# Fixing expert 0 as the first item of a mixture-of-experts stage, with its weights loaded ahead of the routing

## The reference, cut to what matters

```python
mod = jax.nn.silu(c) @ w_mod[l] + b_mod[l]          # six vectors of 1024: shift, scale, gate, twice
x = x + gate1 * rms_norm(hybrid_mixer(h, ...), g_post_mix[l])
h = rms_norm(x, g_pre_ffn[l]) * (1.0 + scale2) + shift2
logits = (xt @ router_w + router_b)                  # 256 x 32
top_v, top_i = lax.top_k(logits, 4)
gates = jax.nn.softmax(top_v, axis=-1)
# for each expert e, over the rows idx that picked it:
gu = xb @ w_gate_up[e] + b_gate_up[e]
act = x_glu * jax.nn.sigmoid(1.702 * x_glu) * (x_lin + 1.0)
out += gate * (act @ w_down[e] + b_down[e])
x = x + gate2 * rms_norm(y, g_post_ffn[l])
```

## Time and profile before

| | |
|---|---|
| median of 3 runs | 2647.13 us (2645.96 to 2648.38) |
| the profiled execution | 2651.04 us, its span 2648.6 us |
| mean granted TensorE clock | 0.98 of full speed |
| PE, DVE, ACT busy | 2439.9, 1115.0, 825.8 us |
| MoE weights moved | 384 loads of 1 MB |
| first MoE load issued | at 259.5 us of the span |
| last item's result read | at 1280.0 us |

### The profile page before, as it was taken

The page is one execution under the profiler, slowest core; times in us unless marked ns, Lnnn a source line. Parts: engine busy times, 40 slices in busy tenths (PEclk is TensorE's granted clock), DMA queues, the critical chain, the costliest instruction groups (busy, mean ns, idle before and its releaser), DMA issues.

```text
span 2648.6 us, 31931 instructions
## 1 busy us (share of the span) xinstructions
PE 2439.9 (92%) x10826; PEld 1504.6 (57%) x10826; DVE 1115.0 (42%) x1597; ACT 825.8 (31%) x1227; POOL 147.2 (6%) x212
## 2 busy tenths in 40 slices
PE   8997899999988888888899999899999999999999
PEld 4755333323222222222488777677887887777787
DVE  4556011110111111111455676856556556887554
ACT  2321111111111111111344345434443444345443
POOL 0000010110100010010000000000000000100000
PEclk9998899999999999999999999999999999999999
DMA  8754999999999999999565562453655655534554
GB/s 308 265 183 131 349 411 421 418 421 402 420 421 421 420 411 408 407 413 410 181 202 185 181 194 80 152 198 109 197 186 167 197 185 190 156 119 164 162 188 145
DMA packets 263485, 700.39 MB, mean 264 GB/s; under 512 B 29512, under 2 KB 128240, under 8 KB 213680
## 3 DMA queue, kind: packets, MB, share of 16 engines
q1 hardware_dynamic: 249780, 685.19, 69.8%
q0 software_dynamic: 9504, 8.42, 0.9%
q10 hardware_dynamic: 4124, 5.77, 0.6%
HBM read 706.58 MB, written 23.63 MB: 276 GB/s over the span
## 4 chain that ended last, share of the span: by engine, by line
PE 41%; DVE 6%; ACT 2%; issue 1%; DMA 1%; POOL 0%; POOLq 0%; DVEq 0%; SPq 0%; ACTq 0%
PE bank L694 10%; PE bank L696 10%; PE bank L695 10%; PE bank L1245 3%; PE bank L1246 3%; PE bank L1247 3%; PE bank L844 1%; DVE w_lo L1390 1%; PE bank L786 1%; PE bank L1235 1%; PE bank L868 1%; PE bank L768 1%; DVE X L1646 1%; POOL st_out L2733 0%; DVE extra L1390 0%
## 5 line engine op out<-in xcount | busy, mean ns | idle before, releaser
L1390 DVE TENSOR_TENSOR w_lo<-raw,w_hi 128x1024 fp32r<-128x1024 f32 (+3 forms) x406 | 489.1, 1215 | 340.8 <-ACT w_hi L2381 336.6
L2381 ACT ACTIVATE w_hi<-raw 128x1024 fp32r<-128x1024 f32 (+3 forms) x406 | 426.5, 1056 | 484.7 <-PE bank L696 280.8
L694 PE MATMUL bank<-w_hi,HTh 128*128 128x512 f32 (+1 forms) x1288 | 513.5, 399 | 16.0 <-DVE HTl L1441 8.2
L696 PE MATMUL bank<-w_hi,HTl 128*128 128x512 f32 (+1 forms) x1288 | 503.2, 391 | 0.0
L695 PE MATMUL bank<-w_lo,HTh 128*128 128x512 f32 (+1 forms) x1288 | 503.1, 391 | 0.0
L2060 DVE TENSOR_SCALAR arena<-bank 64x512 f32<-64x512 f32 (+1 forms) x64 | 44.3, 693 | 580.3 <-PE bank L1100 580.3
L694 PEld LDWEIGHTS bank<-w_hi,HTh 128*128 128x128 f32 x1288 | 244.5, 190 | 69.0 <-DVE HTl L1441 12.7
L696 PEld LDWEIGHTS bank<-w_hi,HTl 128*128 128x128 f32 x1288 | 244.4, 190 | 51.8
L695 PEld LDWEIGHTS bank<-w_lo,HTh 128*128 128x128 f32 x1288 | 245.0, 190 | 46.7
L2577 ACT ACTIVATE arena<-bank,TAB 64x512 f32<-64x512 f32 (+1 forms) x64 | 43.8, 684 | 438.5 <-PE bank L1100 438.5
L1099 PE MATMUL bank<-arena,HT_F 128*64 128x512 f32 (+1 forms) x256 | 121.0, 598 | 25.1 <-DMA arena<-in_moe_w 25.1
(11 more groups left out here) (423 smaller groups left out, 3403.0 us busy)
## 6 DMA issues: line engine op xcount, KB each, us to landing
W_F<-in_moe_w SPq DMA_DIRECT2D x128, 1024.0 KB
raw<-in_moe_w SPq DMA_DIRECT2D x64, 1024.0 KB
arena<-in_moe_w SPq DMA_DIRECT2D x64, 1024.0 KB
raw<-in_ffn_w SPq DMA_DIRECT2D x248, 256.0 KB, 2.9
raw<-in_ffn_w_gu SPq DMA_DIRECT2D x164, 256.0 KB, 3.0
raw<-in_w_in SPq DMA_DIRECT2D x76, 512.0 KB, 4.8
H<-in_moe_w SPq DMA_DIRECT2D x32, 1024.0 KB
MIX<-in_moe_w SPq DMA_DIRECT2D x32, 1024.0 KB, 27.5
```

The costliest lines, as they stand in the source:

```text
L694: pe.matmul(acc, xh, wh, start=start, stop=False)
L696: return pe.matmul(acc, xl, wh, start=False, stop=stop)
L1390: dve.tensor_tensor(lo_at(n, c), raw_at(n, c), hi_at(n, c).bitcast(F32), ALU.subtract).then_inc(lo_done, 1)
L2381: act.activation(hi_at(n, c), raw_at(n, c), ACT.Copy).then_inc(hi_done, 1)
```

## The change

1. Item 0 is always expert 0, worked as a small item of 64 rows, whatever it holds. A new column of the `seg` table takes expert 0 out of the small experts; the flag for big ones still counts it (`seg[:, 2:3]` is kept there), so that an expert 0 with more than 64 rows also stands as a big item later.
2. Its 12 loads are moved ahead, out of the loop over items: pairs 0 to 5 in between the last mod tiles in `order`, 6 to 11 behind the store of `H`. The loop on SP then starts at item 1. The slots are dealt out in another order.
3. Its rows aren't gathered from DRAM: PE multiplies `H` by a 0/1 matrix `FIRST_PICK` (16 matmuls), which gives them already turned. POOL's first gather goes.
4. Its body on PE is written out, with the turning of the gates put inside it (`gates_in`).
5. `RUN` is 3, and there is no `n_first`: behind item 0 there are runs of three small items and a big one, then the small ones left.
6. `mods(3)` moves ahead of PE's wait for `routed`. DVE's arithmetic for the order of items is rewritten; `experts` is copied a little later.
7. Behind the stage the scattered results are loaded into the slots 0, 1, 6 and 10.

```diff
-RUN = 4
-MOST_RUNS = 4
+RUN = 3
+MOST_RUNS = 15
-        plan_mods(24, MOD_TILES)
+        plan_mods(24, 28)
+        order.extend(("early", pair) for pair in range(4))
+        for i in range(2):
+            plan_mods(28 + i, 29 + i)
+            order.append(("early", 4 + i))
+        plan_mods(30, MOD_TILES)
...
+            mods(3)
             pe.wait_ge(E("routed"), 1)
...
-            mods(3)
...
+            pe.wait_ge(E("routed"), 2)
+            for k in range(KD):
+                for tt in range(TT):
+                    mm = pe.matmul(bank[7][:, FEW * k:FEW * (k + 1)], H[:, tt, P * k:P * (k + 1)], FIRST_PICK[:, tt, :],
+                                   start=(tt == 0), stop=(tt == TT - 1))
+            mm.then_inc(m_gather, 2)
...
-            with pe.Fori(0, n_first) as it:
-                expert(it, CAP, CAP)
+            expert(0, FEW, FEW, gates_in)
             with pe.Fori(0, n_runs) as run:
-                with pe.Fori(0, RUN - 1) as j:
-                    expert(n_first + run * (RUN + 1) + j, FEW, FEW)
-                expert(n_first + run * (RUN + 1) + (RUN - 1), FEW, CAP)
-                expert(n_first + run * (RUN + 1) + RUN, CAP, CAP)
-            with pe.Fori(n_first + n_runs * (RUN + 1), n_items) as it:
+                with pe.Fori(1, RUN) as j:
+                    expert(run * (RUN + 1) + j, FEW, FEW)
+                expert(run * (RUN + 1) + RUN, FEW, CAP)
+                expert(run * (RUN + 1) + (RUN + 1), CAP, FEW)
+            with pe.Fori(n_runs * (RUN + 1) + 1, n_items) as it:
                 expert(it, FEW, FEW)
...
-            dve.tensor_scalar(FLAGS[:, 0:1], COUNT, float(FEW), seg[:, 2:3], ALU.is_le, ALU.mult)
+            dve.tensor_scalar(FLAGS[:, 0:1], COUNT, float(FEW), seg[:, 4:5], ALU.is_le, ALU.mult)
             dve.tensor_scalar(FLAGS[:, 1:2], COUNT, float(FEW), seg[:, 2:3], ALU.is_gt, ALU.mult)
...
+            def load_early(pair):
+                if pair == 0:
+                    sp.wait_ge(rows_turned, mix_turned[0])
+                elif pair == 2:
+                    sp.wait_ge(lo_done, moe_at)
+                elif pair == 4:
+                    sp.wait_ge(tile_used, G["out1"][-1].tiles[-1].n + 1)
+                elif pair == 6:
+                    sp.wait_ge(E("h2"), TT)
+                elif pair == 7:
+                    sp.wait_ge(tile_used, moe_at)
+                elif pair == 10:
+                    sp.wait_ge(m_gather, 2)
+                    sp.wait_ge(E("h_stored"), 16 * TT)
+                elif pair == 11:
+                    sp.wait_ge(E("gates"), 1)
+                sp.dma_start(moe_slot(pair), I["moe_w"][0:1, pair, :, :].rearrange("e p n -> p (e n)")).then_inc(m_landed[pair], 16)
...
-                    with sp.Fori(0, n_items) as it:
+                    with sp.Fori(1, n_items) as it:
...
-            rows_in(slice(1, 2), 1)
-            pool.wait_ge(m_gather, 2)
-            rows_in(slice(2, 3), 2)
+            rows_in(slice(2, 3), 1)
```

More of the change, by code:

```diff
@@ L82, in shape_constants @@
     first_block = t // N_EXP % 2 == 0
-    seg = np.stack([first_block, ~first_block, t < N_EXP, np.where(t < 2 * N_EXP, expert, 0)], 1)
+    fixed = expert == 0
+    seg = np.stack([first_block, ~first_block, t < N_EXP, np.where(t < 2 * N_EXP, expert, 0), (t < N_EXP) & ~fixed,
+                    first_block & ~fixed, first_block & fixed], 1)
     def angles(inv):
@@ L632, in build @@
         m_selb = sem("moe_bias_pick")
-        def moe_slot(i):
[L637 to L641, removed]
+        router_part = place_of[G["router"][0].tiles[0].n] // 2
+        apart = 1 - router_part
+        w_slots = [W_F32[:, 2 * j:2 * j + 2, :].rearrange("p a b -> p (a b)")
+                   for j in (apart, 2 + apart, router_part, 2 + router_part)]
+        PAIRS_IN = (0, 1, 6, 10)
+        def moe_slot(i):
+            return (MIX[:, :, :].rearrange("p a b -> p (a b)"), arena_at(MO + D, 2 * TILE),
+                    raw[:, 0:2, :].rearrange("p a b -> p (a b)"), raw[:, 2:4, :].rearrange("p a b -> p (a b)"),
+                    *w_slots[0:2], arena_at(0, 2 * TILE), *w_slots[2:4], HT_F32[:, 1, :, :].rearrange("p a b -> p (a b)"),
+                    H[:, :, :].rearrange("p a b -> p (a b)"), PRPT[:, 0:2 * TILE])[i % MOE_SLOTS]
         def moe_raw(t):
@@ L1003, in _ @@
             gemm("out1", rows_of=(MIX, "mix1"), tail=())
+            mix_turned.append(rows[0])
             mods(8)
@@ L1043, in _, with gates_in @@
             pe.matmul(b[:, 0:2 * N_EXP], NATT, HOLDS[:, 1:65], start=True, stop=True).then_inc(unit_done, 1)
[L1044 to L1050, removed]
             pe.wait_ge(unit_read, unit[0])
             pe.wait_ge(E("zeroed"), 1)
-            pe.wait_ge(mod_read, len(MOD_BANK))
-            pe.wait_ge(m_rows, 16)
-            pe.sem_inc(m_used, MOE_TILES - 16)
+            def gates_in(k):
+                if k == 4:
+                    pe.wait_ge(E("gates"), 1)
+                    turn([GATES[:, tt, :] for tt in range(TT)])
+                if k == 7:
+                    turned_all()
+                    pe.wait_ge(E("last_picked"), 1)
+                    pe.matmul(bank[4 + group[0] % 2][:, 0:S], SEL_LAST, GATET, start=True, stop=True).then_inc(turned, 1)
+                    group[0] += 1
+                    last_gate_group.append(group[0])
             def turn_rows_in(many, half):
@@ L1079, in expert, with up @@
                 high_at = (0, P - many) if many < P else None
-                def up(half):
+                def up(half, between=None):
                     glu, lin = bank[2 + 2 * half][low, :], bank[3 + 2 * half][high, :]
@@ L1094, in up @@
                         if t == 15:
-                            pe.wait_ge(m_rows, it * 16 + 32)
+                            pe.wait_ge(m_rows, it * 16 + 16)
+                        if between is not None:
+                            between(k)
                         if t % 2 == 0:
@@ L1130, in expert @@
                 pe.wait_ge(m_selb, it + 1)
-                up(0)
+                up(0, between)
+                if between is not None:
+                    turned_all()
+                    pe.wait_ge(mod_read, len(MOD_BANK))
                 up(1)
@@ L2004, in _ @@
[L2004 to L2008 removed]
+            step(dve.tensor_scalar(RUN_IS, ramp[:, 1:1 + FEW_RUNS], N_RUNS, None, ALU.is_le))
@@ L2009, in _ @@
+            mark(dve.tensor_scalar(HOLDS[:, 2:65], ramp[:, 2:65], ITEM, None, ALU.is_equal), "items")
+            dve.scalar_tensor_tensor(N_ALL, RANKS[:, 3:4], 1.0, N_RUNS, ALU.add, ALU.add)
+            step(dve.tensor_scalar(N_ROOM, N_RUNS, float(RUN + 1), 2.0, ALU.mult, ALU.add))
             dve.tensor_copy(NRUNS[:, :], N_RUNS)
-            mark(dve.tensor_tensor(NITEMS[:, :], RANKS[:, 3:4], N_BIG, ALU.add), "n_items")
+            step(dve.tensor_tensor(N_ALL, N_ALL, N_ROOM, ALU.max))
+            mark(dve.tensor_copy(NITEMS[:, :], N_ALL), "n_items")
@@ L2897, in _ @@
                         sp.dma_start(h_dram.ap()[P * tt:P * (tt + 1), :], H[:, tt, :]).then_inc(E("h_stored"), 16)
-                    sp.wait_ge(lo_done, moe_at)
-                    sp.wait_ge(E("h_stored"), 16 * TT)
+                    for pair in range(6, MOE_SLOTS):
+                        load_early(pair)
                     sp.wait_ge(E("n_items"), 1)
```

115 lines of the change are left out of this document (56 added, 59 removed).

## The result

The changed kernel takes 2661.02 us, the median of 4 runs (2657.89 to 2663.97), against 2647.76 for 4 runs of the kernel before on the same chip: a ratio of 1.0055, 95% interval 1.0042 to 1.0067 (the quotient of the two medians alone is 1.0050; ratio and quotient can differ by so much, in the fifth experiment by 0.0015). It is slower by 13 us. The forecast was 2658 in a range of 2647 to 2667. The profiled execution took 2663.97 us, its span 2662.1 (before: 2651.04 and 2648.6).

What follows compares the result with a forecast made beforehand. The MoE stage was taken as bound by its weight loads. Expert 0's second visit cancels the loads saved; +0.8 us from the start and d = 10.5 give +11.3 us, so the median goes from 2647.1 to 2658, range 2647 to 2667.

Steps and rivals of the forecast that it cites:

- The bound: MoE stage: bound by its stream of weight loads, 2.61 us a load and 31.38 us an item.
- Expert 0 worked twice: Loop over items: expert 0's 70 rows bring it back as a big item, 33 items, taking back the whole 31.4 us.
- The throttling by a big first item: Start of the load stream: a big item 0 frees slots slowly and costs 10.1 us, which a small first item removes.
- The wait for mod tiles: Turn of H's second half: early pairs ahead of mod tile 30 on SP's queue delay it by 9.0 us.
- I take 1.5: PE's turn and router product: 1.5 us more for a possibly lower clock, out of up to 3.5.
- Net 0: mods(3) ahead of the counts: gain of 1.2 us, of which longer DVE steps take 1, so nothing.
- d: How much later the gates end, and pair 11 goes: 9.0 + 1.5 = 10.5 us.
- So I give 1.5 us (0 to 4): Start of item 0 on PE: time from pair 11 going until PE's first used pair opens slots for item 1.
- The picking: PE's 16 matmuls picking expert 0's rows: 6.6 us, covered by the wait for DVE with 1 us to spare.
- the second: Rival on the mod tiles: they come nearly in time, d is 0 to 3, time 2648 to 2651; chance 0.15.
- The third: Rival: expert 0 has 64 rows or less, no second visit, 2627; chance 0.12 with a branch of earlier gates, 2641.
- The fourth: Rival: clock stays low through turn, router, picking and item 0's first pairs, picking's cover gone, 2664; chance 0.15.

Runs made afterwards that it cites:

- the fifth experiment: Changed kernel with expert 1 fixed as item 0, early pairs behind all mod tiles, and early release of the linear bank: 2617.81 us, ratio 0.9901.
- experiments 1 to 5 and 7: Runs from the changed kernel; without own line: pairs behind mod tiles plus early linear-bank release, 2649.26 us; runs of four small items instead of three, 2662.93 us.
- experiment 8: Changed kernel with all twelve loads of item 0 issued only behind the wait for the list of experts: 2668.30 us, ratio 1.0076.
- The fourth: Changed kernel with expert 1 (6 rows) fixed as item 0 in place of expert 0 (70 rows): 2631.02 us, ratio 0.9941.
- experiment 1: Changed kernel with expert 0's pairs 0 to 5 sent behind all mod tiles instead of between them: 2650.63 us, ratio 1.0009.
- Experiment 6: Kernel before with only mods(3) moved ahead of PE's wait for the top four: 2645.04 us, ratio 0.9993.
- Experiment 2: Changed kernel with DVE's first release of m_lin_read moved up to just behind the count of items: 2658.76 us, ratio 1.0042.

## Why the prediction was right, point by point

**The bound: right.** 747 to 1290 us has a DMA share of 1.00 at 408 GB/s. In the changed kernel and experiments 1 to 5 and 7, the time from the loop's first load to the last item's result is the number of items in the loop times 31.38 us and 6.4 to 7.4 over; in the eighth, counted from item 0's first load, 5.4 over. The fourth takes one item away and gets 30 to 32 us back.

**Expert 0 worked twice: right**, 30 results of 64 rows and 3 of 128, and 396 loads; it takes back the whole of the removed transfer.

**The throttling by a big first item: right in size, its cause not isolated.** Forecast 10.1 us; before, the stream needed 1280.0 - 259.5 - 32 x 31.38 = 16.3 over, and now from 278.12 on 7.4 over, 8.9 less; experiments 6 and 8 give 10.4. But the forecast calls PE's wait of 6.7 us for POOL's gather "outside the stream" and worth nothing. By the working in experiment 8 the late start, of which this wait is the larger part, is one of the two things that the throttling needs, so part of what the forecast gives to the small first item may be the removed gather's. No run took the gather out and left the first item big.

**The wait for mod tiles: right.** Forecast 9.0, measured 9.54 us from the mod row, and 9.5 less in experiment 1. It is the delay that comes out if the transfers go in the order in which they were issued, at the 405 to 417 GB/s and DMA shares of 1.01 and 1.03 measured there; the landing of a single tile isn't in these rows. This agrees with what the Trainium skill states (DMA: Bandwidth & Descriptors, section "Queues, rings and completion order"), that each engine consumes a queue's ring in order. Sharing evenly, which the forecast put at half the delay, would have shown 4 to 5 us.

**The clock ahead of the counts, and `mods(3)`: wrong, to the good.** The step "I take 1.5" for a clock at its lower level and "Net 0" for `mods(3)` failed. The granted clock was 0.62 in 232 to 241, during and behind the wait for tiles, but 1.00 in 246 to 254, where it was 0.58 before. So turn and router product lost nothing, and the three mod matmuls, priced by me at the 5.34 us of a low clock, took 2.84. From the second turn to the end of `gates` it is 268.15 - 243.54 = 24.6 us instead of 266.03 - 237.16 = 28.9. Experiment 6 shows it alone: 24.7. `gates` end 46.6 us from the mod row where 51.8 was forecast (41.3 and d = 10.5): d is 5.3. The Trainium skill's warning (TensorE: Matmul & The Clock Gate, section "HAM oscillation — how this bites in real kernels"), that idle gaps put the clock back, fits the 0.62 measured around the two waits, but the 3.5 us that I drew from it as the far case weren't paid.

**The first load of the loop: wrong, to the bad.** "So I give 1.5 us (0 to 4)" is the step that failed worst: from the end of `gates` to the loop's first load are 278.12 - 268.15 = 10.0 us, where I had 0.3 + 1.5. Two things are in it. PE doesn't reach item 0 with pair 11: its wait for `m_lin_read` is released by DVE at its loop's start, behind `gates` and two more operations, and item 0 begins at 272.15, 4.0 us later. I had looked at what stands ahead on PE, and not at who first raises each semaphore that item 0 waits for. Then PE needs 6.0 us until the first slot opens, since its clock is at the lower level (0.50 in 268 to 280). The idle time didn't put it there: it fell from 1.00 to 0.64 and 0.50 between 254 and 260 us, while PE picked expert 0's rows, busy all the time from 256 to 260 by the rows above. Six rounds of two matmuls, the bias product among them, are 0.9 to 1.0 us apart each, where they are 0.43 at full clock. Experiment 2 takes 4.3 us of the first part and none of the second: 265.65 to 271.62 is 6.0 too, with 2.35 us of idle time ahead of it and the clock at 0.50 in 254 to 268. Even at the full clock six rounds would have been some 2.6 us, more than my 1.5.

**The picking: right.** 5.75 us for 32 instructions where 6.6 were forecast; DVE is what the matmuls behind it wait for (1.28 us at 262.41, its row L1059). **The tail: right**, 0.3 us for 0.

**The sum.** 11.3 forecast, less 5.2 for the gates, plus 8.2 for the first load, less 1.4 in the stream behind it: 12.9 from the mod row, as measured. The 1.4 comes from a term too many: the 2.6 us for pair 11's own transfer stand in the sum beside the time until the next load, though the two pass together (10.0 us here, more than enough for it), while the rest came out at 7.4 instead of 6.2. The landmarks look better than they are, as the shift of 3.2 us helps: the loop's first load, forecast near 278, is at 278.12, but at 281.3 without the shift; the last item, forecast near 1291, is at 1289.71, or 1292.9. The gates, forecast near 276.5, are at 268.15, or 271.3. That the number was close is in part luck: two errors, 5.2 us one way and 8.2 the other, largely cancelled. Of the rivals, the second fell with the wait for tiles. The third was right in its mechanism and decided by the 70 rows. The fourth had the low clock in four places: it was low during the picking and item 0's first pairs, and it was not during the turn and the router product. Nor was the picking's cover gone (PE still waits 1.28 us for DVE).

What stays open: why the clock came back after the few matmuls between the waits for mod tiles, and why it fell while PE picked rows and stayed low until about 280 us. Only its levels were read. Open too is how the 10.4 us divide between a big first item and its late start.

## What to carry to other kernels

A prefetch placed ahead of a bound stream gains only what the stream's next load moves forward. Here that load was tied to the consumer's first step and not to the transfers, so filling an idle stretch of DMA time opened another one behind it; look for the first load that can't be sent, and count back from it. On an in-order queue that serves in order, put small urgent loads first: six expert loads among the mod tiles cost 9.5 us, and behind them none of it. A piece of work pinned to a fixed place has to be taken out of the general list for every input that can occur, or it is paid twice, here some 31 us.

## What the runs showed of the hardware

The same three mod matmuls cost 5.34 us or 2.84 by where they stand: behind a wait of 2.51 us for DVE and the counts (granted clock 0.58 in 246 to 254 us, before), or directly behind the router's busy stretch (1.00 in 238.5 to 242, experiment 6). Filling an idle gap of PE with work that had to be done anyway thus gained twice.

The clock level can cost more at the head of a stage than in it: item 0's first six rounds took 6.0 us in the changed kernel and in all seven experiments built on it, 0.9 to 1.0 us each, against 0.43 from 281 us on. Whether 2.35 or 6.7 us of idle time stood right ahead made no difference; in both traces looked at for it the clock was at 0.50 before the idle time began (0.50 in 258 to 260 in the changed kernel, 0.50 in 254 to 268 in experiment 2).

A PE that the profile calls busy can lose its clock: in 256 to 260 us of the changed trace PE's busy time is 4.00 of 4.00 us, with 26 small matmuls, and the granted clock goes from 1.00 to 0.64 and then 0.50.
